# Two column sums at a time: moving the modulation's small TensorE matmuls to the end of every second unit

## What is computed

```
def swiglu_ffn(x, w_in, w_down):
    h = x @ w_in
    g, u = h[..., :FFN_HIDDEN], h[..., FFN_HIDDEN:]
    return (jax.nn.silu(g) * u) @ w_down
...
    c_act = jax.nn.silu(c)
    for l in range(DEPTH_2):
        mod = (c_act @ mod_w[l] + mod_b[l])[:, None, :]
        sh1, sc1, g1, sh2, sc2, g2 = jnp.split(mod, 6, axis=-1)
        h = _rmsnorm(x, norm1_g[l]) * (1.0 + sc1) + sh1
```

## Time and profile before

| | us |
|---|---|
| median of 3 executions | 2419.61 (2419.35 to 2431.77) |
| the profiled execution | 2422.34 |
| its span, first to last instruction | 2420.5 |
| up projection of layer 0, sum 0 to sum 21 | 498.10 to 736.23 |
| up projection of layer 1, sum 24 to sum 45 | 1413.38 to 1651.11 |

### The profile page before, as it was taken

How to read it: one execution, slowest core, us unless ns; L and a number is a source line. 1 busy time by engine, 2 the same in 40 slices (tenths; PEclk the granted TensorE clock), 3 DMA queues, 4 the chain that set the end, 5 groups by cost and what they waited for, 6 DMA issues and landing times.

```text
span 2420.5 us, 47668 instructions
## 1 busy us (share of the span) xinstructions
PE 2317.2 (96%) x18858; PEld 2134.7 (88%) x18862; DVE 1246.4 (51%) x2504; ACT 1010.3 (42%) x1555; POOL 160.8 (7%) x186
## 2 busy tenths in 40 slices
PE   7999999999999989889999999999989998999998
PEld 7966899899999978756899989999969787999997
DVE  5467344455553146999453455553154644656412
ACT  4556254243332143756353343332153535555413
POOL 1000100100000040135100100000030000000000
PEclk9999999999999999899999999999999999999999
DMA  6333242344552222100242235543212202333220
GB/s 161 82 74 83 83 146 69 87 112 132 137 149 99 102 63 70 37 19 1 70 157 70 71 105 136 150 130 122 87 44 87 76 18 70 89 103 96 95 104 35
DMA packets 307592, 219.02 MB, mean 90 GB/s; under 512 B 42698, under 2 KB 294544, under 8 KB 307472
## 3 DMA queue, kind: packets, MB, share of 16 engines
q1 hardware_dynamic: 255792, 189.30, 26.2%
q10 hardware_dynamic: 49920, 25.17, 4.0%
q0 software_dynamic: 1760, 2.88, 0.4%
HBM read 207.56 MB, written 2.10 MB: 87 GB/s over the span
## 4 chain that ended last, share of the span: by engine, by line
PE 90%; ACT 5%; DVE 3%; issue 1%; DMA 0%; POOL 0%; SPq 0%; DVEq 0%; ACTq 0%; POOLq 0%
PE bank L637 72%; PE bank L779 5%; PE bank L749 3%; PE bank L713 3%; PE bank L879 1%; PE bank L1094 1%; PE bank L937 1%; PE bank L929 1%; ACT ST L1510 1%; PE bank L1143 1%; ACT XH L1180 1%; ACT XT L1354 1%; ACT BI L1180 1%; DVE SC L1963 1%; ACT WH L600 0%
## 5 line engine op out<-in xcount | busy, mean ns | idle before, releaser
L637 PE MATMUL bank<-XH,WH 128*128 128x256 f32 x3568 | 1003.3, 281 | 33.0 <-DVE XL L1828 24.4
L637 PE MATMUL bank<-XL,WH 128*128 128x256 f32 x3568 | 996.7, 279 | 0.0
L637 PE MATMUL bank<-XH,WL 128*128 128x256 f32 x3568 | 996.5, 279 | 0.0
L637 PEld LDWEIGHTS bank<-XH,WH 128*128 128x128 f32 x3568 | 678.7, 190 | 41.9 <-issue 32.1
L637 PEld LDWEIGHTS bank<-XH,WL 128*128 128x128 f32 x3568 | 676.1, 189 | 0.0
L637 PEld LDWEIGHTS bank<-XL,WH 128*128 128x128 f32 x3568 | 675.1, 189 | 0.2 <-issue 0.2
L604 DVE TENSOR_TENSOR WL<-RAW,WH 128x2048 fp32r<-128x2048 f32 x172 | 394.2, 2292 | 525.8 <-ACT WH L600 525.8
L600 ACT ACTIVATE WH<-RAW 128x2048 fp32r<-128x2048 f32 x172 | 328.6, 1911 | 445.7 <-PE bank L637 445.5
L637 PE MATMUL bank<-HH,WH 128*128 (+1 forms) x1056 | 295.2, 280 | 0.9 <-DVE HF L1908 0.9
L637 PE MATMUL bank<-HH,WL 128*128 (+1 forms) x1056 | 294.9, 279 | 0.0
L637 PE MATMUL bank<-HL,WH 128*128 (+1 forms) x1056 | 294.9, 279 | 0.0
(11 more groups left out here) (304 smaller groups left out, 3168.3 us busy)
## 6 DMA issues: line engine op xcount, KB each, us to landing
RAW<-in_ffn_w_in SPq DMA_DIRECT2D x88, 512.0 KB, 5.0
MB<-in_mod_w ACTq DMA_DIRECT2D x48, 512.0 KB, 5.2
RAW<-in_ffn_w_down SPq DMA_DIRECT2D x44, 512.0 KB, 3.9
RAW<-in_ffn_up SPq DMA_DIRECT2D x44, 512.0 KB, 4.5
RAW<-in_xa_w_kv SPq DMA_DIRECT2D x32, 512.0 KB, 4.4
RAW<-in_ffn_down SPq DMA_DIRECT2D x22, 512.0 KB, 4.0
RAW<-in_xa_w_q SPq DMA_DIRECT2D x16, 512.0 KB, 4.0
RAW<-in_xa_w_o SPq DMA_DIRECT2D x16, 512.0 KB, 4.4
```

The costliest lines, as they stand in the source:

```text
L637: mm = nc.tensor.matmul(out_ap[:, cols], l, moving, start=(start and n == 0 and k == 0), stop=(stop and n == len(parts) - 1 and k == len(o ...
```

## The change

`two_sums` takes the place of the lambda that did one sum behind each unit. It does nothing behind units with j = 1. Behind units with j = 0 (units 0, 2, ..., 20) it waits once for `mod_out` m, that is for all columns below m, and then does the sums of columns m and m+1, each with its own wait for its products. DVE's `hidden` does the columns m and m+1 one after the other in its even units and none in its odd ones. The products and the loads keep their places. For the last two columns of a layer one wait for `mod_out` stands ahead of both sums. The number of sums, 48, is the same.

```diff
                     pe.wait_ge(mod_step, m * 9 + 9)
-                    if not isinstance(m, int) or m >= 2:
-                        pe.wait_ge(mod_out, m - 1)
                     nc.tensor.matmul(bank[4 + par][:, 0:1], ACC[:, par, 0, :], ONES[:, 0:1], start=True,
                                      stop=True).then_inc(mod_mm, 1)
+                def two_sums(i, j):
+
+                    if j % 2 == 0:
+                        m = i + MOD_N * f
+                        if not isinstance(m, int) or m:
+                            pe.wait_ge(mod_out, m)
+                        for par in range(2):
+                            mod_sum(m + par, par)
                 if f < DEPTH:
-                    wide_stage(f"ffn_in{f}", xpairs(), fill,
-                               behind=lambda i, j: mod_sum(i + MOD_N * f, j % 2))
+                    wide_stage(f"ffn_in{f}", xpairs(), fill, behind=two_sums)
...
                     norm_sums(norm, (y_free, DC * f + DC), bank[1], bank[0])
+                    pe.wait_ge(mod_out, MOD_N * f + MOD_N - 2)
                     for m in (MOD_N - 2, MOD_N - 1):
...
                     if f < DEPTH:
-                        mod_column(i + MOD_N * f, j % 2)
+                        if j % 2 == 0:
+                            for par in range(2):
+                                mod_column(i + (MOD_N * f + par), par)
                         mod_products(i + (MOD_N * f + 2), j % 2)
```

## The result

The change makes the kernel a little slower, by less than 1% but clear of the noise. The median of 11 executions is 2441.16 us (2432.40 to 2447.12), that of the kernel before, measured beside it, 2419.68 us (2412.58 to 2431.80); the ratio given with the measurement is 1.0074, with a 95% interval from 1.0050 to 1.0099 (the bare medians give 1.0089). The prediction said 2419.6 us and a range up to 2429. The profiled execution of the kernel after took 2446.03 us with a span of 2443.5 us, 23.0 us more than that of before.

What follows compares the result with a forecast made beforehand. The prediction took PE, busy 96% of the span, to bound the kernel. Sums, waits, DVE and pace each added 0, giving 2419.6 us against the median, with a range from 2409 to 2429 us.

Steps and rivals of the forecast that it cites:

- What bounds the kernel: Whole kernel: PE busy 96% of 2420.5 us; at the sums, only PE's own issue and pace move time.
- The sums' own cost: At the sums behind the units: a pair costs 0.45 us, like two lone sums, so pairing saves 0.00 us.
- The waits and DVE: Up projections: merged waits cost 0, second sum keeps 2.9 us of slack, DVE's two columns add 0 on the path.
- The pace: Up and down projections of the first block: sums may turn PE's fast or slow state; net 0 under either reading.
- (a): Pair turns pace twice or keeps it: layer 0 gains 4.4 us, layer 1 loses 4.4; net 0, favoured 3 to 2.
- (b): Pair turns pace once: layer 0's down projection loses 4.4 us, layer 1's gains 4.4; net 0.
- the four transposes: Early in the kernel: four short matmuls with loads cost 0.45 us extra and showed the same pace on both sides.
- two full products: Burst of two f32 products, also four loads: 73 matmuls in 8 us before, 70 after; evidence for one turn.
- bounds on the slots: At the 22 pairs: at most one slot of 0.11 us each, 2.4 us in all, gained or lost.
- pace lost downstream: Rival: second block's up projection, all fast before, comes out slow; 8.8 us more, 2428.4 us, chance 0.11.
- The Trainium skill's rule: Matmuls on a warm clock: one gap, 262 cycles for 256 columns, whatever stood before; by it, no change at all.

Runs made afterwards that it cites:

- the second profiles: The changed kernel and the kernel before, each run once more unchanged for a second trace: 2433.89 us after, 2422.57 us before.
- couples 3 apart: Changed kernel with each pair's second sum moved 3 regular matmuls later, into the next unit; timed in both layers: median 2409.96 us, ratio 0.9940 to the kernel before.

## Why the prediction was wrong, point by point

- **What bounds the kernel: right.** PE's pace is what moved in the change's own stages. The two paces, their size and their being a state that is carried along were read correctly before.
- **The sums' own cost: right.** 0.45 us forecast for a pair, 0.45 us measured. The loads have their slots whether they stand together or not.
- **The waits and DVE: right.** No idle time at the sums. The last products that the second sum behind unit 6 needs, and that sum, in the timelines of DVE and PE after, against the earlier trace rows:

```profile
562.70 0.29 DVE L1863 TENSOR_TENSOR ACC<-ACC 128x128 f32<-128x128 f32 x1
```

```profile
566.17 0.50 PE L984 MATMUL bank<-KC,ACC 128*128 128x1 f32 x4
```

  The products end at 562.99 and the pair starts at 566.17: 3.2 us of slack, where 2.9 were forecast. DVE's waits for PE in layer 0, 75.7 us before, are 79.8 now, since PE is slower:

```profile
DVE HF L1899 <- PE bank L637: 79.8, 22, 4.4
```

- **The pace, the step that failed.** The prediction gave two readings of what a pair does to the state, (a) it turns it twice or not at all, (b) it turns it once. It summed each to 0. The pair does neither: from fast it leaves slow, from slow it leaves slow. Both readings treated a group of sums as something that turns or keeps. A group that sets the pace was not among them, and it is the only kind that doesn't cancel out: a map that is one to one, as (a) and (b) are, gives back in one place what it takes in another; one that sends both paces to slow only takes. The term of 0 measured 8.5 us in layer 0 and 4.2 us in layer 1 (8.6 and 7.9 us between the second profiles, in which the kernel before entered layer 1 fast).
- **Its evidence.** I leaned to (a) by the four transposes, "short" as the sums, with the same number of loads. They are 128 columns wide, and a pair of 128 columns kept the fast pace where a pair of one column did not. And their row was one throw: in 3 of the 11 profiles that come to them fast they leave slow. The other row at hand, two full products, had shown fast turning to slow; over all profiles they do turn the pace, from both sides, and still a pair of one column does not. In the one trace at hand neither row showed the pace coming in from the other side, so neither could tell "turns" from "sets". The bounds that I drew for the unknown cost were bounds on the slots (2.4 us each way); the unknown map had none of its own. The worst map, slow everywhere, was a simple sum: 4.4 us for the 11 fast units of layer 0, 4.4 for its fast down projection and 4.4 for the 11 fast units of layer 1: 13.2 us, so 2432.8 us (at 4.44 ns a step it is 0.43 us a unit where I had read 0.40, and 14 us). That should have been a rival with a chance, since nothing in the profile spoke against it.
- **The rival "pace lost downstream"** put 8.8 us on the second block's up projection. It came out slow in the profiled execution and fast in the next. No run here shows it to be a consequence of the change; it is a part of the 23.0 us in that one profile and of the spread between runs.
- **The Trainium skill's rule**, "TensorE: Matmul & The Clock Gate", section "Back-to-back issue gap", gives for a matmul of 256 columns taken by itself one gap on a warm clock, 262 cycles, and names none that depends on what stood ahead. The traces differ: 113.33 and 117.78 ns at a granted clock of 1.00, by what stood ahead. Here the measurement decides.

## What to carry to other kernels

In a kernel that PE bounds, read the distance of starts, not the busy time or the clock: a difference of 4% hid here between steps of 113 and 118 ns. Do not put short f32 matmuls next to each other between long runs of regular ones; one regular matmul between two of them was enough to turn the worst pace into the best, for nothing (in stages that came in fast; from a slow one only three between were tried). When a small instruction seems to switch a state, ask of every new arrangement what it does from each side, and price the map in which it always ends on the wrong one. And look for the same group in a second profile before taking its row for a rule.

## What the hardware showed that was not expected

Regular matmuls of this kernel (128x128 weights that change each time, 256 moving columns) run at 113.33 or 117.78 ns a step, with the granted clock at 1.00, for thousands of steps on end, and in the up projections the choice is made by the short sums, in the same way each time. Elsewhere it can fall either way behind the same instructions: behind the four transposes, and behind a start that comes 0.05 us late, which left the fast pace in 7 profiles and the slow one in 4. It also turned where one kind of product followed another with no late start. Over the kernel the slow steps cost up to 49 us, or 2%. What in PE holds this state was not shown. That the number of loads decides is excluded, since two sums adjacent and two apart have the same; so is a plain parity, which pairs of one column and couples 3 apart break. Whether some offset between the weight loads and the matmuls is kept, which the group of short instructions shifts, would fit but was only thought, not tested.
